# Moving the sample blocks of two output projections, the order of a stage's first keys, and when square sums are taken

## The reference

```python
for layer in range(DEPTH):
    hp, hs = rms_norm(xp, norm_mix[layer]), rms_norm(xs, norm_mix[layer])
    if layer % N_MIXERS == 0:
        yp, sp = retention_mixer(hp, pos_p, s0, RET_CHUNK, *rw)          # prompt
        ys, ss = retention_mixer(hs, pos_s, state_ret[r], xs.shape[1], *rw)  # samples
    else:
        yp, kp, vp = swa_prompt(hp, *aw)
        ys, kn, vn = swa_sample(hs, cache_swa_k[a], cache_swa_v[a], *aw)
    xp, xs = xp + yp, xs + ys
    xp = xp + swiglu(rms_norm(xp, norm_ffn[layer]), w1, w3, w2)
    xs = xs + swiglu(rms_norm(xs, norm_ffn[layer]), w1, w3, w2)
y_prompt, y_sample = rms_norm(xp, norm_final), rms_norm(xs, norm_final)
```

## Time and profile before

| | us |
|---|---|
| median of three runs (lowest, highest) | 2001.91 (1998.64, 2004.72) |
| the profiled execution, its own time | 1995.12 |
| span of its slowest core, from first to last instruction | 1994.1 |
| spans of the 8 cores | 1970.7 to 1994.1 |
| TensorE matmul busy | 1861.9 (93%) |
| VectorE busy | 875.6 (44%) |
| ScalarE busy | 679.8 (34%) |
| GpSimd busy | 222.2 (11%) |
| share of the chain of waits that lies on TensorE's matmuls | 79% |
| granted TensorE clock, mean of the slowest core | 0.980 |

### The profile page before, as it was taken

The page is one execution under the profiler, slowest core; times in us unless marked ns, Lnnn a source line. Parts: engine busy times, 40 slices in busy tenths (PEclk is TensorE's granted clock), DMA queues, the critical chain, the costliest instruction groups (busy, mean ns, idle before and its releaser), DMA issues.

```text
span 1994.1 us, 29657 instructions; the slowest of 8 cores (1970.7 to 1994.1 us)
## 1 busy us (share of the span) xinstructions
PE 1861.9 (93%) x10183; PEld 857.4 (43%) x10183; DVE 875.6 (44%) x1549; ACT 679.8 (34%) x1066; POOL 222.2 (11%) x363
## 2 busy tenths in 40 slices
PE   4999989999999999999879999999999889899997
PEld 1444444344444333343334444545454533455553
DVE  3565533434356663434555554332223556422225
ACT  3544433322224742123344443221022366210112
POOL 0111111010111010101001111101011010011010
PEclk9999999999999999999989999999999999899999
DMA  9434556797996259998636665755345240254352
GB/s 194 73 64 80 93 77 109 197 203 174 208 200 134 43 101 218 204 208 205 141 110 118 104 93 82 128 71 73 53 65 80 44 64 1 33 82 72 51 73 95
DMA packets 214257, 220.27 MB, mean 110 GB/s; under 512 B 45632, under 2 KB 168896, under 8 KB 214080
## 3 DMA queue, kind: packets, MB, share of 16 engines
q0 software_dynamic: 128112, 114.08, 40.2%
q1 hardware_dynamic: 86000, 104.30, 17.7%
HBM read 277.10 MB, written 48.89 MB: 163 GB/s over the span
## 4 chain that ended last, share of the span: by engine, by line
PE 79%; DVE 7%; DMA 6%; issue 4%; ACT 3%; POOL 0%; DVEq 0%; SPq 0%; ACTq 0%; POOLq 0%
PE ps L579 79%; DVE rt L603 2%; DMA wr<-w 1%; DMA x_62<-xTp 1%; DMA uT_64<-g_73 1%; DMA S_2_109<-st_in 1%; DMA wr<-wa 1%; DVE stat L858 1%; DMA x_63<-xTp 1%; PE ps L584 0%; DVE h_44 L606 0%; ACT sq L595 0%; DVE x_62 L606 0%; DVE h_45 L606 0%; DMA yTp<-x_62 0%
## 5 line engine op out<-in xcount | busy, mean ns | idle before, releaser
L579 PE MATMUL ps<-h_44,wr 128*128 128x512 bf16 x1824 | 416.2, 384 | 14.0 <-DMA wr<-wa 8.4
L579 PE MATMUL ps<-h_45,wr 128*128 128x512 bf16 x1824 | 415.3, 381 | 1.2 <-ACT s_104 L595 1.2
L579 PEld LDWEIGHTS ps<-h_44,wr 128*128 128x128 bf16 x1824 | 175.8, 99 | 231.7 <-issue 35.3
L579 PEld LDWEIGHTS ps<-h_45,wr 128*128 128x128 bf16 x1824 | 174.2, 98 | 219.3 <-issue 21.9
L259 POOL DMA_DIRECT2D wr<-w x152 | 112.9, 746 | 1012.3 <-PE ps L579 904.1
L579 PE MATMUL ps<-aT_103,wr 128*128 128x512 bf16 x704 | 159.0, 381 | 1.2 <-DVE aT_136 L603 1.1
L595 ACT ACTIVATE s_104<-ps 128x512 f32<-128x512 f32 x88 | 52.4, 596 | 310.9 <-PE ps L579 283.5
L579 PE MATMUL ps<-aT_105,wr 128*128 128x512 bf16 x704 | 157.6, 379 | 0.0
L603 DVE TENSOR_TENSOR aT_103<-s_104,ps 128x512 bf16<-128x512 f32 x88 | 60.4, 688 | 216.7 <-PE ps L579 195.9
L603 DVE TENSOR_TENSOR aT_105<-s_106,ps 128x512 bf16<-128x512 f32 x88 | 60.5, 688 | 210.2 <-PE ps L579 181.5
L579 PE MATMUL ps<-wr,h_44 128*128 128x512 bf16 (+1 forms) x576 | 130.0, 374 | 6.0 <-ACT rstd_57 L595 3.6
(11 more groups left out here) (294 smaller groups left out, 2152.7 us busy)
## 6 DMA issues: line engine op xcount, KB each, us to landing
wr<-w POOLq DMA_DIRECT2D x88, 512.0 KB, 7.1
wr<-wa POOLq DMA_DIRECT2D x24, 1024.0 KB, 11.6
wr<-w POOLq DMA_DIRECT2D x64, 352.0 KB, 7.0
wr<-wo POOLq DMA_DIRECT2D x16, 512.0 KB, 8.4
S_0_107<-st_in SPq DMA_DIRECT2D x16, 512.0 KB, 6.2
S_1_108<-st_in SPq DMA_DIRECT2D x16, 512.0 KB, 6.9
S_2_109<-st_in SPq DMA_DIRECT2D x16, 512.0 KB, 6.3
S_3_110<-st_in SPq DMA_DIRECT2D x16, 512.0 KB, 6.6
```

The costliest lines, as they stand in the source:

```text
L579: self.S.op("pe", lambda e: e.matmul(out, lhsT, rhs, start=start, stop=stop, skip_group_check=skip), r, w, dur=k * max(0.1, self.n(out) * ...
```

## The change

Five edits. The sample blocks of retention's output projection follow ta's pieces and not tb's, so six of the eight are in the list that is merged with the retention of tb; the sample blocks of attention's output projection run between ta's and tb's. The weight blocks are given back by tb's pieces. Half 1 begins its retention in the `lead` order too. Pieces of the sample attention get a third item. `norm_tick` issues a square sum when the plan has the square for half a microsecond. The output of the samples is stored by two DMAs of half the size.

```diff
@@ norm_tick
-            while j.mm and self.S.t_read(self.sqb[j.mm[0][0]]) <= t:
+            while j.mm and self.S.t_read(self.sqb[j.mm[0][0]]) <= t - 0.5:
                 self.norm_do_mm(j)
@@ ret_layer: wo_p
-                    if ti == 1 and not wo_rider:
+                    if ti == 1:
                         self.ring.done(("wo", dm))
...
-                if ti == 1 and wo_rider:
+                if ti == 0 and wo_rider:
                     def fs(dm=dm):
...
-                        self.ring.done(("wo", dm))
@@ ret_layer
-        X.run(P(0, 0, s == 0))
+        X.run(P(0, 0, True))
@@ att_layer: wo1_s
-                    self.ring.done(("wo1", dm))
@@ att_layer: SC
-            pcs.append((1, prep))
+            pcs.append((1, prep, self.need(lambda: sq_[1])))
-                pcs.append((1, lambda b4=b4: trs(b4)))
+                pcs.append((1, lambda b4=b4: trs(b4), self.need(lambda: kw[1], [bank[2 + b4 % 2]])))
-                pcs.append((1, lambda kvh=kvh: news(kvh)))
+                pcs.append((1, lambda kvh=kvh: news(kvh), self.need(lambda: skd[1] + sq_[1], [bank[4], bank[5]])))
-                pcs.append((2, lambda b4=b4: scs(b4)))
+                pcs.append((2, lambda b4=b4: scs(b4), self.need(lambda: [kT[1][b4]] + qS[1], [bank[2], bank[3]])))
-                pcs.append((5, lambda kvh=kvh: nd(kvh)))
+                pcs.append((5, lambda kvh=kvh: nd(kvh), self.need(lambda: [pN[1][kvh]] + pC[1], [bank[6], bank[7]])))
@@ att_layer, half 1
             X.run(w0[6:])
+            X.run(wo1_s())
             norms[0]()
-            X.run(wo1_p(1, False))
-            X.run(wo1_s())
+            X.run(wo1_p(1, True))
@@ program: end of the last ffn
-                    return self.norm_begin(scx, 4, NB4, True, lambda: self.dma(
-                        "sp", DR["yTs"].rearrange("(kc p) t -> p kc t", p=128), self.xs[:, :, :], self.xsb, [], "xs"))
+                    def out():
+                        for k in (0, 4):
+                            self.dma("sp", DR["yTs"].rearrange("(kc p) t -> p kc t", p=128)[:, k:k + 4, :], self.xs[:, k:k + 4, :],
+                                     self.xsb[k:k + 4], [], f"xs{k}")
+                    return self.norm_begin(scx, 4, NB4, True, out)
```

## The result

The changed kernel ran at 1986.72 us (median; 1986.29 to 1988.19), the kernel before beside it at 2000.28 (1993.46 to 2004.72): a ratio of 0.9936, interval 0.9907 to 0.9966. That is 12.8 us, near the 13.4 of the sum. (Medians, ranges, ratios and mean spans leave out executions in which one die showed a lower clock than the other.) Both intervals hold a gain of 7 to 10 us. The direction was right and the time was met, but the 13.4 us of the sum lie outside the second interval (3.2 to 10.0 us): the sum is too large by some 6 us, and the terms show that it is one of them. That the first comparison came so near the sum is luck: the same two kernels gave half of it when more runs were taken.

What follows compares the result with a forecast made beforehand. TensorE, busy 1861.9 of 1994.1 us, was taken as the bound, so only its waits and slow clock could give time. Seven terms summed to 13.4 us, from 2001.9 to 1988.5, said as 1988; range for 8 in 10: 1974 to 2003.

Steps and rivals of the forecast that it cites:

- A: Sample blocks of attention's output projection, moved ahead of tb's: fewer waits behind VectorE's scalings, net gain 4.8 us, ends -2 and 7.9.
- rivals 1: Waits in A, C and E only change their name, VectorE and ScalarE setting the pace: 1999 us, chance 0.20.
- Rival 2: Three norms open at once leave tb's projections one bank, each piece waiting for its addition: 2009 us, chance 0.10.
- F: Square sums issued later, throughout the kernel: fewer TensorE waits for squares, gain 1.5 us, ends 7.1 and -6.
- B: Start of the last ffn: the slow clock goes if the stretch ahead is full, gain 2.5 us, ends 5.5 and -1.4.
- I leave a wait of about 2 us: Last ffn's start: tb's norm ends behind the first Silu, needs the same two table changes, so about 2 us of wait stays.
- C: Sample attention: third items put projections of tb where results are late, gain 3.0 us with the clock, ends 8.7 and -2.
- The 3.2 us said to stay: Sample attention: waits of 0.85, 1.04 and 1.27 us taken to remain once the six projections of tb are spent.
- D: Sample blocks of retention's output projection, six moved into the merge: two waits for squares go, gain 0.5 us, ends 2.9 and -2.
- E: First keys at half 1's start: waits for the rotated key go behind four v pieces, gain 0.8 us, ends 2.7 and -3.
- G: Samples' output at the end, stored in two halves: gain 0.3 us, ends 0 and 1.1.
- Rival 3: Fuller stretches keep TensorE at 2.4 GHz, so more clock loss comes back: 24 us in all, 1978 us, chance 0.08.

Runs made afterwards that it cites:

- the second interval: The changed kernel, no edit, measured again beside the kernel before with more runs: 1991.7 us against 1999.1, ratio 0.9967 (0.9950 to 0.9984).
- the ten kernels with the same lists there: The kernels with the changed kernel's lists in attention's output projection, whatever else was edited: that stage takes 59.66 to 60.42 us.

## Why the prediction was right in sign and too large

**A, 4.8 us: right in size.** The stage gave 4.3. On core 2 the eight blocks run from 1681.09 to 1687.33, 6.2 us (under 6.5 said; the sum had 5.5), the ffn starts 26.0 us behind the first (26 said, 29.75 before), and tb's projection takes 18.5 us, below the 19.5 that would have spoken for rivals 1 and 2. But it is not A's alone: with F in place A brings 2.2 of it, or 1.4 by the highest of the ten kernels with the same lists there.

**B, 2.5: too small by 2.2; the step that failed is "I leave a wait of about 2 us".** The clock came back as said, and by A as said: full level on all eight cores, where the ffn's first 10 us had 0.68 to 0.76 before and so lost 2.4 to 3.2 us (half the length of the stretches recorded at 1.2 GHz). The wait didn't stay: tb's last sums moved behind ta's first pieces, and none waits for the rstd. The table change that I feared is there, hidden (ScalarE, core 2, after):

```profile
1707.77 1.28 ACT L593 ACT_TABLE_LOAD   x1
1709.10 0.60 ACT L595 ACTIVATE s_104<-ps 128x512 f32<-128x512 f32 x1
...
1710.24 1.28 ACT L593 ACT_TABLE_LOAD   x1
1711.53 0.60 ACT L595 ACTIVATE rstd_57<-ps 128x512 f32<-128x512 f32 x1
```

Each next activation starts within 0.05 us of the load's end. The drain that the Trainium skill (ScalarE: Activation LUTs, What ACT_TABLE_LOAD costs) adds is not in this trace either.

**C, 3.0: right in kind, 3.8 in the stage and 3.9 when undone.** On core 7 the four waits of 5.24 us and one of 0.31 became 2.46, so 3.1 us are theirs; the rest may be the clock, which no run separates. The 3.2 us said to stay are these 2.46, in other places: the two for the key copies at the front remain, and behind the sixth projection the releaser is VectorE.

**D, 0.5 forecast, 5.9 lost: the step that failed, and with 6.4 us more than the distance between 13.4 and the table's 7.6.** The other errors nearly cancel, and that is luck: B gave 2.2 more than said, C 0.8 more, A 0.5 less, and the rows of E, F and G together 1.8 less. The sum of D was not sound as it stood: its own rows, 0.56 + 0.77 - 1.5, give -0.2, and the 0.7 to reach 0.5 (waits of A's kind that no longer occur) has no row. But the sign hung on something else. I had written that the plan counts 1.6 us for a block that takes 0.9 and believes squares ready too soon, and used it only to explain two old waits. I didn't ask what it does where the block now stands. There it placed three sums about 1.5 us too early, in a merge that had no idle time to lose; "the merge with retention still without idle time" failed. With the price corrected for these blocks alone, and nothing else moved, 5.1 of the 5.9 us came back. The bound of -2 was too near as well: I bounded the lateness of a sample's addition on VectorE, and the late thing was a sum over the first tile's squares.

**E, 0.8, and F, 1.5: not separate terms.** The stage of E gave 1.1, within the scatter, and with F in place E's order is worth nothing that can be seen. "No wait ahead of the key transposes" failed (1.53 for the gate). F's own gains in attention (3.2) and in the first ffn (1.5) are given back at the start of half 1, behind that ffn and in the tail. In half 0 F did take from the waits for squares about what I said, 7.1 to 4.6 us on core 7 (8.2 without F), but the end of half 0 is too uneven to show it. "Waits for squares at half of 23.4" failed: 14.7 to 19.5 us on the eight cores, 17.6 in the mean (21.2 before). I had charged 0.5 for norms that end a piece later; the tail alone shows 1.5 from the last ffn matmul to the last sum (1.56 us before, 3.06 after).

**G, 0.3: 0.9,** within the ends of 0 and 1.1.

**Rivals.** Rival 1, waits with a new name, is what the start of half 1 shows (E); A and C kept their gains. Rival 2 (three open norms) did not occur: the longest wait for an addition in tb's projection of attention is 0.38 us on core 2, where it said 2.4 us a piece. Rival 3 came for the last ffn only; clock dips stay at the start of half 1 (0.83 from 1003 to 1023 on core 7) and behind the sample attention (0.70 from 1607 to 1617).

## What to carry to other kernels

When an order comes from a planner, compare its price for the moved operation with the trace before anything else: a block priced at 1.6 us and taking 0.9 misplaces not itself but whatever the plan thinks will be ready behind it. A gain in a starved stretch was paid out twice here, in the waits and in the clock of the stretch behind; a loss in a full stretch has nothing to hide in. The gains of two edits that remove the same wait must not be added.

## What the runs showed of the hardware

Sixteen 128-column matmuls in a row ended 1.06 us after the first began, with 0.22 for a single one, so one begins each 0.056 us ((1.06 - 0.22)/15). The Trainium skill (TensorE: Matmul & The Clock Gate, Back-to-back issue gap) gives 0.081 for a sustained stream with weight loads and 0.056 for the bare gap; the rows here, with a weight load for each matmul, agree with the second. By the first, an estimate, a block would be priced at 1.3 us, still above the 0.9 measured.

In the traces of the two kernels the cores differ by 17 and 21 us at the end of half 0, and by under 0.1 over the first ffn of half 1 (268.8 us before, 266.8 after). So on this kernel a stage of half 1, from retention's output projection on, tells some 1 us when it is read on eight cores, where the ratio of the times, over some ten runs, has an interval of 3.5 us to either side.
